# Attention branch A of a hybrid encoder step: logits and biased maximum three units ahead instead of two, the exponential two ahead as before

## The reference, cut to what matters

```
logits = einsum('bthd,btkd->bthk', qa, k_sel) * HEAD_DIM**-0.5 + bias
logits = where(valid, logits, NEG_INF)
probs  = softmax(logits)
out    = einsum('bthk,btkd->bthd', probs, v_sel)      # 8 heads, HEAD_DIM 64
```

## Time and profile before

| | |
|---|---|
| time, median of 3 runs | 1879.21 us (1875.88 to 1880.67) |
| the profiled execution | 1873.19 us, its span 1871.2 us |
| TensorE matmul busy | 1795.1 us, 96% of the span |
| TensorE weight loads busy | 1708.4 us, 91% |
| VectorE, ScalarE, GpSimd busy | 942.5, 645.3 and 469.8 us |
| mean granted TensorE clock | 0.988 |

### The profile page before, as it was taken

One profiled execution on the slowest core, in us unless ns is written; L12 is line 12 of the kernel. 1 busy time (PEld: TensorE's weight loads), 2 busy tenths in 40 slices (PEclk: granted clock), 3 DMA queues, 4 the chain that ended last, 5 costly groups with the idle time before them and its releaser, 6 DMA issues.

```text
span 1871.2 us, 30256 instructions
## 1 busy us (share of the span) xinstructions
PE 1795.1 (96%) x11176; PEld 1708.4 (91%) x11176; DVE 942.5 (50%) x2291; ACT 645.3 (34%) x1254; POOL 469.8 (25%) x269
## 2 busy tenths in 40 slices
PE   7799999999989998999999999999999999999996
PEld 2688999999978887778999999999999999999995
DVE  1657888899155555555655453332323232323234
ACT  3445566631155444544322240403030312121212
POOL 0521222224211101121223232223232322233330
PEclk9899999999999998999999999999999999999998
DMA  8611224242442223653443111111111111111112
GB/s 281 164 43 26 67 87 114 93 127 78 122 122 60 71 71 83 184 160 115 140 146 99 45 35 46 46 46 45 45 45 34 45 45 45 45 45 44 37 43 96
DMA packets 179321, 153.47 MB, mean 82 GB/s; under 512 B 20240, under 2 KB 162016, under 8 KB 178688
## 3 DMA queue, kind: packets, MB, share of 16 engines
q1 hardware_dynamic: 175328, 137.31, 25.5%
q10 hardware_dynamic: 3920, 15.19, 2.0%
HBM read 127.34 MB, written 25.19 MB: 82 GB/s over the span
## 4 chain that ended last, share of the span: by engine, by line
PE 87%; DVE 5%; ACT 3%; DMA 2%; issue 2%; SPq 0%; POOL 0%; DVEq 0%; ACTq 0%
PE psum L812 68%; PE psum L1087 5%; PE psum L1078 3%; PE psum L1114 2%; PE psum L936 2%; PE psum L969 2%; PE psum L1050 1%; PE psum L1051 1%; PE psum L850 1%; DMA ada_c<-in_w_ada 1%; PE psum L1054 1%; DVE h_f L1606 1%; DVE u_lo L1989 1%; DVE logit L1801 1%; DMA out<-y_out 1%
## 5 line engine op out<-in xcount | busy, mean ns | idle before, releaser
L812 PE MATMUL psum<-h_hi,w_hi 128*128 128x362 f32 (+2 forms) x1440 | 475.2, 330 | 2.5 <-DVE h_lo L1967 1.6
L812 PE MATMUL psum<-h_lo,w_hi 128*128 128x362 f32 (+2 forms) x1440 | 474.6, 330 | 0.0
L812 PE MATMUL psum<-h_hi,w_lo 128*128 128x362 f32 (+2 forms) x1440 | 474.0, 329 | 0.0
L753 POOL CAST w_hi<-w_raw 128x1024 fp32r<-128x1024 f32 x112 | 124.5, 1112 | 1033.7 <-PEq L816 887.8
L755 POOL TENSOR_TENSOR w_lo<-w_raw,w_hi 128x1024 fp32r<-128x1024 f32 x112 | 281.8, 2516 | 9.0
L812 PEld LDWEIGHTS psum<-h_hi,w_hi 128*128 128x128 f32 x1440 | 271.5, 189 | 3.3 <-DVE h_lo L1967 1.9
L812 PEld LDWEIGHTS psum<-h_lo,w_hi 128*128 128x128 f32 x1440 | 271.9, 189 | 0.0
L812 PEld LDWEIGHTS psum<-h_hi,w_lo 128*128 128x128 f32 x1440 | 271.8, 189 | 0.0
L1951 DVE SCALAR_TENSOR_TENSOR xT<-psum,modT,xT 128x364 f32<-128x364 f32 (+3 forms) x288 | 136.2, 497 | 265.4 <-PE psum L812 265.4
L812 PE MATMUL psum<-u_hi,w_hi 128*128 128x362 f32 (+1 forms) x768 | 253.4, 330 | 3.2 <-DVE u_lo L1989 3.2
L1523 ACT ACTIVATE u_relu<-u_relu,b_up 128x364 f32<-128x364 f32 (+3 forms) x128 | 63.4, 519 | 553.6 <-DVE u_relu L2001 553.6
(11 more groups left out here) (288 smaller groups left out, 2868.2 us busy)
## 6 DMA issues: line engine op xcount, KB each, us to landing
w_raw<-in_w_in SPq DMA_DIRECT2D x32, 512.0 KB, 4.2
ada_c<-in_w_ada SPq DMA_DIRECT2D x32, 512.0 KB, 4.0
w_raw<-in_w_up SPq DMA_DIRECT2D x32, 512.0 KB, 4.2
w_raw<-in_w_down SPq DMA_DIRECT2D x32, 512.0 KB, 3.4
zT_scratch<-z_out ACTq DMA_DIRECT2D x27, 544.0 KB, 2.7
q_raw<-zT_scratch SPq DMA_DIRECT2D x32, 272.0 KB, 5.1
gate<-zT_scratch SPq DMA_DIRECT2D x16, 544.0 KB, 4.6
ada_w<-in_w_ada SPq DMA_DIRECT2D x4, 2048.0 KB, 9.1
```

Source lines behind the costliest of these rows:

```text
L753: pl.tensor_copy(w_hi[slot][:, :], w_raw[slot][:, :]).then_inc(sem("w_hi_made"), 1)
L812: ins = pe.matmul(bank(b, n), w[:, k, wc], x[:, a, c0:c0 + n], start=(m == 0 and p == 0), stop=(m == len(wk) - 1 and p == 2))
```

## The change

`ahead` gives the unit three ahead in branch A too; TensorE's `logits` and VectorE's `biased` use it. A new function `exp_ahead` keeps the old rule, two ahead in branch A and three in B, and ScalarE's `probs` uses it. Three units are prepared ahead of the loop on TensorE and VectorE, two on ScalarE. As unit n+3 shares its `logit` buffer with unit n, `biased` now waits for the last transpose of the unit three back in every case but where that is a sample unit, which has its own buffer. No work is added or left out.

```diff
         def ahead(n):
+
+            return units[n + 3] if n + 3 < (NA if n < NA else NU) else None
+
+        def exp_ahead(n):
 
             k = n + (2 if n < NA else 3)
             return units[k] if k < (NA if n < NA else NU) else None
@@ TensorE
             logits(units[0])
             logits(units[1])
+            logits(units[2])
             for u in units:
@@ ScalarE
-                if ahead(n):
-                    probs(ahead(n))
+                if exp_ahead(n):
+                    probs(exp_ahead(n))
@@ VectorE, in biased(u)
                 s, n = ring(u), u["n"]
-                if n >= 3:
-                    g = units[n - 3 if u["br"] == "a" else max(n - 4, NA - 1)]["groups"][-1][0]
+                past = n - 3 if u["br"] == "a" else max(n - 4, NA - 1)
+                if past >= 0 and not (u["br"] == "a" and units[past]["blk"] is None):
+                    g = units[past]["groups"][-1][0]
                     dv.wait_ge(sem(f"turned{g % 2}"), g // 2 + 1)
@@ VectorE
             biased(units[0])
             biased(units[1])
+            biased(units[2])
             for u in units:
```

## The result

The changed kernel takes 1856.45 us in the median of 4 runs (1856.04 to 1859.32), the kernel before beside it 1879.48 us (1875.88 to 1880.67). These medians stand 23.0 us apart; the ratio on record is 0.9891 [0.9876, 0.9905], which would be 20.5 us. Measured again the median was 1857.05 us and the ratio 0.9903 [0.9887, 0.9919], and on a third occasion 1858.16 us and 0.9903 [0.9886, 0.992]; a ratio of 0.9903 on the 1878.28 us of the kernel before is 18.2 us, while the medians stood 21.2 and 19.8 us apart. The profiled execution took 1856.75 us, its span 1854.8 us, 16.4 us less than the span before.

What follows compares the result with a forecast made beforehand. TensorE, busy nearly all the time, was taken as the bound, its waits caused by exponentials held for nmax on ScalarE. 12.2 + 1.3 + 3.4 = 16.9 us, less 1.9, gives 15: 1879.2 to 1864.2 us, range 1859.5 to 1875.

Steps and rivals of the forecast that it cites:

- the places in the pairs and pair 0: Branch A: TensorE's waits at three places per pair of heads, 9.7 us, and pair 0's cached keys, 2.5 us, go.
- the most: Upper limit of the gain: 12.2 + 1.3 + 3.4 = 16.9 us, before 1.9 us is taken off.
- the anchor: Median of the kernel before, 1879.2 us, 6.0 us above its profiled execution, from which 15 us were taken.
- start: Start of branch A: one more `logits` fills 1.3 us of TensorE's 2.41 us wait for the first exponential; 1.1 us stays.
- clock: TensorE's two clock falls in branch A, at the start and in pair 3, go: 3.4 us; bounds nothing to 3.4 us.
- the first two: TensorE's waits before the transposes of L1106 (3.9 us) and before the weigh (3.3 us), both claimed to go.
- the third: Transposes waiting 0.94 us for ScalarE's copy behind two held exponentials; with its like 2.1 + 0.4 us, claimed to go.
- The deduction: 1.9 us taken off for small waits coming back: L1106's transposes, 0.3 us three times, and the queries' loads.
- ScalarE's own queue as the limit: Rival, chance 0.18: ScalarE's exponential and high parts in a row, not nmax, set two waits; gain 8 us, 1871.2 us.
- The change doesn't do what it says: Rival, chance 0.16: VectorE's `biased` still needs same-iteration logits, so only the start gives, 3 us: 1876.2 us.
- The queries' loads: Slower rival, chance 0.04: at `q_hi` ScalarE waits for seven q_raw loads, e.g. 6 us slower, 1885.2 us.
- The waits go, the clock doesn't give: Rival, chance 0.20: branch A's waits go but clock falls elsewhere or was absent in most runs; 12 us, 1867.2 us.

Runs made afterwards that it cites:

- the hold of nine exponentials: Changed kernel, ScalarE's nine exponentials in front of the outputs' high parts (pairs 1 to 3) held for the next unit's maximum: 1863.1 us, 0.9925.
- the full hold: Changed kernel, every exponential of unit n+2 in branch A also waiting for the maximum of unit n+3: 1872.87 us, 0.9977.
- the start of before: Changed kernel, unit 2's logits and maximum made inside iteration 0 instead of ahead of the loop: 1857.62 us, 0.9901.
- the exponential behind: Kernel before, ScalarE's exponential of n+2 moved behind the keys' and outputs' high parts in 13 iterations, look-ahead still two: 1862.42 us, 0.9924.

## Where the prediction was right, and where it failed

The median came out at 1856.45 us, 7.8 us below the 1864.2 us and below the whole range. The mechanism was right; the step that failed is the sum, in two of its terms. The main one is the 12.2 us for the places in the pairs and pair 0, which measured 14.9 us. It also made 16.9 us "the most" and so set the lower end of the range. The other is the 1.9 us taken off for thin margins, which measured 1.1 us. Together they are 3.5 of the 7.8 us; the other 4.3 us aren't in branch A as the profiled executions show it (see the anchor below). By the weight loads' rows the terms measured:

| term (us) | predicted | measured |
|---|---|---|
| places in the pairs and pair 0 | 12.2 | 14.9 |
| start | 1.3 | 1.3 |
| clock | 3.4 | 3.4 |
| waits that come back | -1.9 | -1.1 |
| sum | 15.0 | 18.5 |

**The places** (the step of the first two parts that takes TensorE's waits from the earlier trace rows). Each was found rightly: the hold of nine exponentials brought the first two back, and a new order on ScalarE took them away; the third was explained in keeping with the full hold, but not tested by itself. Their price was read from the matmuls' rows, which stand for 14.6 us where the weight loads' rows stand for 18.3. What went is 4.3 + 4.5 + 2.2 + (5.6 - 2.6) + (0.8 - 0.3) + 0.4 = 14.9 us; the 2.6 is the start.

**The start** was right, 2.6 to 1.3 us, and 1.1 us was forecast to stay.

**The clock** was right in these executions: both falls went. But the reason given, that one of two equal waits had no fall and so falls are partly chance, isn't borne out for these places: the kernel before fell at the same two in both of its executions. It is borne out elsewhere, by the fall at the end of branch B that one of three executions of the changed kernel had after the same waits. Nor does the length of the wait decide: 2.4 us had no fall behind it in one experiment, and 1.3 us has one in pair 3 and none in the pairs 1 and 2. Which condition decides stays open; no kernel here isolates it.

**The deduction** took 1.9 us for margins that seemed thin. One of them was overrun, for 0.9 us, and at the first place, where y_tok is 0.06 us ahead of TensorE, none came back. It was a guess without a row behind it, 0.8 us too large here; the overrun alone is 0.4 to 1.4 us in three executions. The other 0.2 us of the 1.1 stand before unit 2's own logits ahead of the loop, for which the prediction took nothing.

**The range** ended at 16.9 us of gain, called "the most", and 2.4 us for the spread (1879.2 - 16.9 - 2.4 is 1859.9 us, not 1859.5). It took one view's price of the waits as the upper bound; by the other the same sum is 14.9 + 1.3 + 3.4 = 19.6 us. Branch A's 18.5 us lies between. Even 18.5 us, taken off 1879.2, give 1860.7 us, still inside the range: what put the median outside it is the next point.

**The anchor.** 15 us were taken from a median of three, 1879.2 us, which stood 6.0 us above the profiled execution. The 56 executions of the kernel before timed beside the experiments have a median of 1877.4 us, so 1.8 us of the 4.3 are an anchor that was high by chance. From 1877.4 us, 18.5 us lead to 1858.9 us; the changed kernel's 14 executions have a median of 1856.7 us. These last 2 us or so are in no stretch of a profiled execution, and their cause stays open; falls of 1.7 us outside branch A, which come in some executions, are of that size. The 16.4 us between the two profiled executions is an understatement: the one before was a low one, and the changed kernel's had the fall at the end of branch B, so that what lies behind branch B was 1.8 us longer, and what lies ahead of branch A 0.5 us. Branch A's 18.5 us is the measure that doesn't depend on this.

**The rivals.** ScalarE's own queue as the limit fell: unheld, it is in time. "The change doesn't do what it says" fell by the 5.3 us for nmax. The queries' loads were there, in their place and by their mechanism, and with their sign, ScalarE waiting over 2 us for q_raw at two loads of seven; TensorE paid at one of them, 0.4 to 1.4 us. "The waits go, the clock doesn't give" fell for branch A, where both falls went.

## What to carry to other kernels

Look in an in-order queue for the instruction that is held longest, and ask not what it is worth itself but who waits for what is queued behind it: ScalarE, with half of its time free, stood 74 us for a maximum; putting that hold back alone cost 15.6 of the 18.5 us, and a new order on that engine alone gave 14.9 of them. The cure is distance between the producer and the held instruction, not depth on every engine; pushing all three engines one further gave 3.7 us. And a wait that is removed may have covered a load: issue that load first, or the gain turns into it.

## What the runs showed of the hardware

- TensorE's idle time before matmul rows is less than before weight loads, 14.6 against 18.3 us here, and the latter adds up better. Branch A's length less the waits before weight loads and less what the clock cost (1.7 us for each fall) was 191.5 to 191.7 us in the kernel before, twice, in the changed one, three times, and with the start of before. It was 192.1 us with the exponential behind, 191.2 with all held, 190.8 with nine held and 190.2 with the exponential three ahead. By the matmul rows the same sum is 196.3 us in the kernel before and 194.2 in the changed one.
- In branch A the granted clock fell to the lower of its two levels (1.2 of 2.4 GHz) for long enough to cost about 1.7 us, at the same two places in both executions of the kernel before, after waits of 2.4 and 1.3 us; a wait of 2.4 us was followed by no fall in the kernel with the exponential behind. With all exponentials held one fall cost 3.4 us, after a wait of 1.85 us.
- The same kernel with the same waits (0.74 and 1.07 us) fell at the end of branch B in one of its executions, for 1.7 us, and stayed at 1.00 in the other two.
